# Expert job 0 in four quarter tiles with 32 slots, and its first three weight pieces in a buffer of their own

## The reference, cut to what matters

```python
def moe_swiglu(h, w_router, b_router, w_gate, w_up, w_down):
    logits = (h @ w_router).astype(jnp.float32) + b_router.astype(jnp.float32)
    top_vals, top_idx = lax.top_k(logits, TOP_K)
    top_w = jax.nn.softmax(top_vals, axis=-1)
    gates = jnp.sum(jax.nn.one_hot(top_idx, N_EXPERTS, dtype=jnp.float32)
                    * top_w[..., None], axis=-2).astype(h.dtype)
    out = jnp.zeros_like(h)
    for e in range(N_EXPERTS):
        out = out + gates[..., e:e + 1] * swiglu(h, w_gate[e], w_up[e], w_down[e])
    return out
```

## Time and profile before

| what | value |
|---|---|
| median of 3 runs | 1481.5 us (1481.41 to 1485.14) |
| profiled execution | 1486.44 us, span 1484.3 us |
| PE busy | 1399.5 us (94%) |
| DVE, ACT busy | 733.3 us (49%), 624.4 us (42%) |
| moved by DMA | 449.25 MB, mean 303 GB/s over the span |
| chain that ended last | PE 80%, DMA 8%, DVE 4%, ACT 3% |

### The profile page before, as it was taken

The page is one execution under the profiler, slowest core; times in us unless marked ns, Lnnn a source line. Parts: engine busy times, 40 slices in busy tenths (PEclk is TensorE's granted clock), DMA queues, the critical chain, the costliest instruction groups (busy, mean ns, idle before and its releaser), DMA issues.

```text
span 1484.3 us, 19444 instructions
## 1 busy us (share of the span) xinstructions
PE 1399.5 (94%) x7520; PEld 923.9 (62%) x7520; DVE 733.3 (49%) x923; ACT 624.4 (42%) x838; POOL 9.7 (1%) x24
## 2 busy tenths in 40 slices
PE   6988999999999988989999799999999999999987
PEld 5866788888789563347653276345876346876325
DVE  5665554444576355026620166206896108885005
ACT  5565544444473252026520155005775006774004
POOL 1000000000000000000000000000000000000000
PEclk9988999999999999999999999999999999999999
DMA  9922555555422385999879998999999999999992
GB/s 328 375 100 88 189 170 186 183 185 185 169 86 64 97 343 205 410 408 413 314 291 412 406 406 322 350 407 409 415 406 410 408 405 412 413 406 412 412 405 102
DMA packets 137356, 449.25 MB, mean 303 GB/s; under 512 B 8972, under 2 KB 13159, under 8 KB 124727
## 3 DMA queue, kind: packets, MB, share of 16 engines
q1 hardware_dynamic: 134736, 443.00, 77.9%
q0 software_dynamic: 1072, 3.84, 0.8%
q10 hardware_dynamic: 1462, 1.21, 0.3%
HBM read 441.27 MB, written 2.10 MB: 299 GB/s over the span
## 4 chain that ended last, share of the span: by engine, by line
PE 80%; DMA 8%; DVE 4%; ACT 3%; issue 2%; SPq 1%; ACTq 1%; DVEq 0%
PE psum L1006 18%; PE psum L587 18%; PE psum L589 17%; PE psum L588 17%; DMA weight_ring<-in_moe_w_gate 5%; DMA weight_ring<-in_ple_w_gate 2%; PE psum L1165 2%; DVE weight_lo L1810 1%; SPq L417 1%; PE psum L1180 1%; ACT weight_hi L1331 1%; ACTq L402 1%; DMA weight_ring<-in_attn_w_qkv 1%; PE psum L628 1%; PE psum L938 1%
## 5 line engine op out<-in xcount | busy, mean ns | idle before, releaser
L1331 ACT ACTIVATE weight_hi<-weight_ring 128x1024 fp32r<-128x1024 f32 x410 | 428.6, 1059 | 263.9 <-PE psum L589 242.2
L1810 DVE TENSOR_TENSOR weight_lo<-weight_ring,weight_hi 128x1024 fp32r<-128x1024 f32 x326 | 391.3, 1223 | 178.7 <-ACT weight_hi L1331 177.6
L1006 PE MATMUL psum<-weight_ring,silu_gate 128*64 128x512 f32 x960 | 216.7, 605 | 6.9 <-issue 6.3
L587 PE MATMUL psum<-weight_hi,act_hi 128*128 128x512 f32 x448 | 180.8, 403 | 11.2 <-issue 5.6
L588 PE MATMUL psum<-weight_lo,act_hi 128*128 128x512 f32 x448 | 178.3, 398 | 0.0
L589 PE MATMUL psum<-weight_hi,act_lo 128*128 128x512 f32 x448 | 178.1, 398 | 0.0
L2380 DVE TENSOR_TENSOR hidden<-silu_gate,psum 128x512 f32<-128x512 f32 (+1 forms) x20 | 12.4, 621 | 306.5 <-PE psum L1006 246.3
L1006 PEld LDWEIGHTS psum<-weight_ring,silu_gate 128*64 128x64 f32 x960 | 68.4, 139 | 139.4 <-issue 135.5
L587 PE MATMUL psum<-weight_hi,job_act_hi 128*128 128x512 f32 x336 | 137.9, 410 | 8.1 <-DVE weight_lo L1810 3.2
L589 PE MATMUL psum<-weight_hi,job_act_lo 128*128 128x512 f32 x336 | 134.3, 400 | 0.0
L588 PE MATMUL psum<-weight_lo,job_act_hi 128*128 128x512 f32 x336 | 134.1, 399 | 0.0
(11 more groups left out here) (353 smaller groups left out, 1397.8 us busy)
## 6 DMA issues: line engine op xcount, KB each, us to landing
weight_ring<-in_moe_w_gate SPq DMA_DIRECT2D x112, 1024.0 KB, 18.2
weight_ring<-in_moe_w_up SPq DMA_DIRECT2D x112, 1024.0 KB, 18.2
weight_ring<-in_moe_w_down SPq DMA_DIRECT2D x112, 1024.0 KB, 15.9
weight_ring<-in_ffn_w_gate SPq DMA_DIRECT2D x14, 1024.0 KB, 5.0
weight_ring<-in_ffn_w_up SPq DMA_DIRECT2D x14, 1024.0 KB, 5.0
weight_ring<-in_ffn_w_down SPq DMA_DIRECT2D x14, 1024.0 KB, 5.0
weight_ring<-in_attn_w_qkv SPq DMA_DIRECT2D x12, 1024.0 KB, 13.7
weight_ring<-in_conv_w_pw SPq DMA_DIRECT2D x12, 1024.0 KB, 5.1
```

The source lines that it names most:

```text
L587: pe.matmul(dst, ahi_, bhi_, start=first, stop=False, **kw)
L1006: ins = pe.matmul(ps[halves[half], bank, :], lhs, raw(u)[:, half * CW:(half + 1) * CW], start=first, stop=last)
L1331: act.activation(whi[:, u % SPLIT, :], raw(u), ACT.Copy).then_inc(hi_done, 1)
L1810: dve.tensor_tensor(wlo[:, u % SPLIT, :], raw(u), whi[:, u % SPLIT, :].bitcast(F32), ALU.subtract).then_inc(lo_done, 1)
```

## The change

Job 0 gets 32 slots (`EXTRA`) in place of 64. A unit is then four matmuls of 128x256 with 32 array columns each, in place of two of 128x512 with 64. The gather, the transposes, the activations and the job table follow the new width: what expert 0 has beyond 32 tokens becomes a job of its own, where it was what lies beyond 64. With 21 tokens for expert 0 the list of jobs stays as it was. `light_scatter(0, ...)` becomes `quarter_scatter`, with 16 matmuls of 32x256 in place of 8 of 64x512.

A second tile, `first_weights` (3 pieces), lies over the `weight_hi` and `weight_lo` buffers, which are idle between the last dense layer and the big job. Pieces 0 to 2 of job 0 go there instead of into the ring, and the ring starts with piece 3. So the ring's pieces 14 to 16 go to slots that were never filled, and wait for nothing of their own. SP issues the three `first_weights` DMAs behind ring piece 16 and ahead of piece 17.

```diff
-        emb1, = overlay(("embedding_1", [P, T, D], F32))
+        emb1, early = overlay(("embedding_1", [P, T, D], F32), ("first_weights", [P, EARLY, 2 * UNIT], F32))
...
             def load(piece, src, j, kt=4):
                 slot = piece % RING
-                if piece >= RING:
+                if j is None and U_MOE // 2 + RING <= piece < U_MOE // 2 + RING + EARLY:
+                    sp.sem_inc(piece_in[slot], 16)
+                elif piece >= RING:
                     sp.wait_ge(lo_done, after(2 * (piece - RING) + 2, JOB, j))
...
+            def first_weights(w):
+                sp.wait_ge(unit_used, U_PROJ1)
+                for i in range(EARLY):
+                    sp.dma_start(early[:, i, :].rearrange("p (t n) -> p t n", t=2),
+                                 w[i * 2 * P:(i + 1) * 2 * P, 0:GW].rearrange("(t p) n -> p t n", p=P)
+                                 ).then_inc(early_in[i], 16)
+
             def wide(at, w, s, j):
+                first = U_MOE // 2
                 for i in range(4):
-                    if j is None and at == U_MOE // 2 and i == X4_PIECE - U_MOE // 2:
+                    if j is None and at + i == first:
                         shifted_copies()
+                    if j is None and at + i < first + EARLY:
+                        continue
+                    if j is None and at + i == first + RING + EARLY:
+                        first_weights(w_first)
...
                 def wide_unit(u, lhs, bank, first, last):
                     wait_raw(u)
-                    for half in range(2):
-                        ins = pe.matmul(ps[halves[half], bank, :], lhs, raw(u)[:, half * CW:(half + 1) * CW],
+                    for g, rows in enumerate(tiles):
+                        ins = pe.matmul(ps[rows, bank, 0:width], lhs, weights(u)[:, g * width:(g + 1) * width],
                                         start=first, stop=last)
                     ins.then_inc(lo_done, 1)
...
+            def quarter_scatter(done, banks):
+                pe.wait_ge(ylo_done, 2 * done + 2)
+                for odd in range(2):
+                    if odd:
+                        pe.wait_ge(sc_first, 1)
+                    for t in range(T):
+                        for q in (odd, odd + 2):
...
-            light_job(0, embedding=True)
+            light_job(0, embedding=True, slots=EXTRA)
```

More of the change, by code:

```diff
@@ L209, in program @@
         piece_in = [sem(f"piece_in{i}") for i in range(RING)]
+        early_in = [sem(f"first_weights_in{i}") for i in range(EARLY)]
         hi_done = sem("hi_done")
@@ L940, in gather_rows @@
                     last.then_inc(rows_ready, 2)
+                elif slots == EXTRA:
+                    for t in range(T):
+                        for q in range(NQ):
+                            last = pe.matmul(ps[q * EXTRA:(q + 1) * EXTRA, bank, 0:HW], sel[:, t, 0:EXTRA],
+                                             hrow[:, t, q * HW:(q + 1) * HW], start=t == 0, stop=t == T - 1)
+                    last.then_inc(rows_ready, 2)
                 else:
@@ L959, in _ @@
             pe.wait_ge(sel_done, 1)
-            gather_rows(LIGHT, 2)
-            gather_transpose(LIGHT, 2, 0, None)
+            gather_rows(EXTRA, 2)
+            pe.wait_ge(rows_done, 2)
+            for k in range(2):
+                last = pe.transpose(ps[:, 2, k * P:(k + 1) * P], rows_x[:, k * P:(k + 1) * P], ident[:, :])
+            last.then_inc(xe_ready, 2)
             pe.sem_inc(ghT_ready, GROUPS)
@@ L1012, in narrow_unit @@
                     for k in range(2):
-                        for half in range(2):
-                            at = k * CW + half * HW
-                            ins = pe.matmul(ps[halves[half], bank, 0:HW], xe[:, 2 * i + k, :], raw(u)[:, at:at + HW],
+                        for g, rows in enumerate(tiles):
+                            n = CW // parts
+                            at = k * CW + g * n
+                            ins = pe.matmul(ps[rows, bank, 0:n], acts[:, 2 * i + k, :], weights(u)[:, at:at + n],
                                             start=i + k == 0, stop=i == 3 and k == 1)
@@ L1021, in light_linear @@
                         if s < 3:
-                            wide_unit(first + unit + i, xe[:, i, :], bank, i == 0, i == KT - 1)
+                            wide_unit(first + unit + i, acts[:, i, :], bank, i == 0, i == KT - 1)
                         else:
@@ L1077, in light_job @@
                         t, half = n % 2, n // 2
-                        pe.matmul(ps[:, n, :], selT[halves[half], t * P:(t + 1) * P],
-                                  ysb[halves[half], 0:CW], start=True, stop=True).then_inc(sc_ready, 1)
+                        pe.matmul(ps[:, n, :], selT[tiles[half], t * P:(t + 1) * P],
+                                  ysb[tiles[half], 0:CW], start=True, stop=True).then_inc(sc_ready, 1)
             def small_job(j):
@@ L1640, in _, with light_job @@
             act.sem_inc(ghThi_done, GROUPS)
-            def light_job(j, last_job=False, between=False, embedding=False):
+            def light_job(j, last_job=False, between=False, embedding=False, slots=LIGHT):
                 first = U_MOE + (HALF if between else 0)
```

75 lines of the change are left out of this document (52 added, 23 removed).

## The result

The change makes the kernel slower. The first timing has a median of 1501.2 us in four executions (1494.3, 1500.1, 1502.3, and a disturbed one of 1768 that the ratio leaves out) against 1481.9 us: 1.0095, 95% interval [1.0066, 1.0124]. The ratios come from all undisturbed executions and are not the quotients of the medians. Three later timings of the same two kernels give 1493.6 against 1485.5 (1.0058 [1.0043, 1.0074]), 1495.0 against 1484.5 (1.0075 [1.006, 1.009]) and 1494.3 against 1484.3 (1.0058 [1.0038, 1.0078]). The forecast was 1488.1, +0.45%, with a range that ended at 1492.0. Direction and mechanism were right, the size too small, and all four medians are above the range.

A forecast was written before the change was run, and what follows sets the result against it. The prediction took the DMA stream, not PE, to set the end of job 0. It added 6.4 us for the later stream and 0.2 for the scatter, +6.6 on the median, giving 1488.1 us (+0.45%), range 1483.0 to 1492.0.

The forecast's parts named there:

- What bounds job 0: Job 0: the DMA stream sets its end, at 2.60 us a piece, not PE, which takes 1.76 us a piece.
- Seven pieces behind the wait: Start of job 0: SP issues seven pieces at 566.7, first_weights last, landing 581.6 to 590.9; piece 17 issued at 594.8.
- From piece 17 to the big job: Rest of job 0: the same 25 pieces at 2.60 us; piece 42 lands at 664.5, big job starts at 667.1.
- What the quarter tiles save counts as zero: Job 0: 38 us of PE time saved lies beside a stream that PE waits for, so it gains nothing.
- Scatter: Job 0's scatter, where PE is the bound: one added PE wait between two halves, +0.2 us (0.1 to 1.2).
- The shift is passed on whole: Behind job 0: all waits are relative, so the later start reaches the kernel's end unchanged, nothing added.
- The base: Whole kernel: the sum was put on the median of the runs, 4.9 us below the profiled execution of 1486.4.
- the term for the stream: Start of job 0: piece 17 lands at 599.6 instead of 593.2, +6.4 us.
- Rival 1: Start of job 0: same step but smaller, clock high or store out of the way sooner; +2 to +4.4 us, 1485; chance 0.18.
- Rival 2: Job 0: PE bounds it after all, so 38 us are saved less 8.8 of later start; 1452; chance 0.02.
- Rival 3: Start of job 0: the early fetch works, landing ahead of 572.8; piece 17 lands 4.5 us sooner, 1477; chance 0.06.
- Rival 4: Job 0: clock stays low throughout, PE falls behind the landings; +11.6 us, 1493.1; chance 0.10.

The follow-up runs named there:

- the quarter tiles alone: The changed kernel with pieces 0 to 2 left in the ring (no early fetch): 1484.1 against 1485.5 us for the kernel before, 0.9998.
- the fillers: Changed kernel plus an unused 128x256 matmul behind each wide unit from job 0's second up stage: 1494.2 us, 1.0069; in two tile-used-twice variants 1482.8 and 1477.6.
- half tiles with early fetch: The kernel before, job 0 still with 64 slots, its first three pieces in first_weights issued behind ring piece 16: 1491.1 against 1485.5 us, 1.0044.

## Why the prediction was right or wrong

**What bounds job 0: right.** The stream sets its end. With quarter tiles the third window above has DMA share 1.03 beside a PE that is busy two thirds of the time.

**Seven pieces behind the wait: right, nearly to the tenth.** T is 0.9 us later than before in this profile. Counted from T of each profile, E0 was forecast at +15.5 and landed at +16.4 (10.9 us behind piece 13 for four pieces, 2.7 each and not 2.56), E2 at +24.8 and +25.0, piece 17's issue at +28.7 in both. The store took 6.1 - 2.5 = 3.6 us of E2's time, inside its bounds; this offset most of what E0 lost. The clock read 0.50 over all four units after E2, as I took it.

**From piece 17 to the big job: right, 0.8 us short.** Piece 17 took 5.1 us to land and not 4.8, and the 25 pieces behind it 65.5 and not 64.9. In the profile on which the sum was made this gives +7.2, over six profiles 7.3 to 7.9, mean 7.5, for a forecast of **6.4: this term was 1.1 too small.** The big job starts 2.6 us behind piece 42, as today.

**What the quarter tiles save counts as zero: right** for the changed kernel; alone they bring piece 42 3.3 us sooner. PE waits for DMAs in every piece, as forecast.

**Scatter: 0.2 forecast, 0.3 measured.** The changed kernel's PE timeline from its first matmul to the next group (670.64 to 671.79, 1.15 us, in the earlier trace rows):

```profile
678.51 0.39 PE L1029 MATMUL psum<-expert_out_hi,one_hot_T_r 32*128 32x256 f32 x2
...
679.32 0.39 PE L1029 MATMUL psum<-expert_out_hi,one_hot_T_r 32*128 32x256 f32 x2
...
679.99 0.41 PE L1225 MATMUL psum<-weight_ring,extra_act 128*32 128x256 f32 x2
```

1.48 us, in two halves of 0.81 and 0.67 us, the wait for the drain in the first.

**"The shift is passed on whole": a step that failed.** Big job to end is 823.2 on the mean of three profiles before and 824.8 on that of six of the changed kernel, +1.6, of which the scatter is 0.3; T itself is 565.7 on the mean of both. Of the rest, 1.0 is the slip of 3 us in two of six profiles; some tenths have no name. With 7.5 that makes 9.1, against 8.1, 10.6 and 10.0 us in the three later timings.

**The base.** The sum on the profiled execution was 1493.0, and the changed kernel's profiled execution took 1494.3. It was set down by 4.9 us to the median of three runs, and later medians of the kernel before lie 3 to 4 us above that. Of the 5.5 to 6.9 us by which the later timings miss 1488.1, this is about half.

**The steps that failed, together.** The base was 2.8 to 4.0 us too low, the term for the stream 1.1 too small (7.5 for 6.4), and "passed on whole" left out 1.4 behind job 0 (1.6 for the scatter's 0.2): 5.3 to 6.5 us, where the later timings miss the forecast by 5.5 to 6.9. The first timing misses it by 13 us. The two terms explain 2.5 of these and the base at most 4; the rest stays open.

**The rivals.** Rival 1 (+2 to +4.4) falls by the profile: the clock was not high when E2 landed. Rival 2 falls by the quarter tiles alone. The Trainium skill, "TensorEngine Tiling (Array Packing)", Theoretical Speedup, gives twice the speedup for 32 that it gives for 64, and the trace agrees on the price of the work (ten units in 4.52 us at full clock, 0.45 each for 0.88), but the kernel got no shorter by it. Rival 3 names what the change could do, and did when its three DMAs were put ahead of piece 13: T + 85.3, 6.6 sooner than before, where it had 4.5; 3.3 of these are the quarter tiles', and 3.4 us showed in the time. Rival 4 falls by the profile (PE waits for DMAs up to its last units) and by the fillers, though the clock went low again and again, as it supposed. The Trainium skill, "TensorE: Matmul & The Clock Gate", HAM oscillation, tells of a kernel whose waits for DMAs send the clock low again and again; the forecast found no such pattern in the trace, and the changed kernel has one, with waits of 0.5 to 1.7 us. Windows of it:

```profile
616.50:623.00 6.50, 4.54 (x40) 1.67 (x44) 0.00 (x0) 0.38 (x1) 0.00 (x0) 0.50 1.01 420
623.50:630.00 6.50, 2.48 (x40) 0.83 (x32) 0.00 (x0) 0.00 (x0) 0.00 (x0) 1.00 1.01 407
630.20:636.80 6.60, 5.36 (x48) 1.67 (x48) 0.00 (x0) 0.00 (x0) 0.00 (x0) 0.50 1.03 405
```

It costs next to nothing (0.4 us at piece 42, by the fillers): even at 0.50 two units take 1.93 us, and a piece takes 2.56.

**Still open.** What the first timing's executions of 1500.1 and 1502.3 did: no profile is of one like them. The mean clock of the second (0.957) is lower than that of any later execution (0.963 and up). Whether the slip at the first small job comes from the change. And what the early fetch, put ahead of piece 13, gives in half tiles: every kernel with the better order had quarter tiles, so their share in it (3.3 us at piece 42) is known from the run of quarter tiles alone.

## What to carry to other kernels

A buffer that is free early gives an early load only if nothing that waits stands ahead of it in the list of the engine that issues it; here, in quarter tiles, the same three DMAs cost 10.8 us behind a waiting one (99.4 for 88.6 to piece 42) and gave 3.3 ahead of it (85.3). Where loads set the end of a stage, count pieces and landings first, and ask of the arithmetic only when it frees a buffer: 38 us of matmul time saved there brought the last landing 3.3 us forward and gave no time that could be measured. And put a sum on the time of the execution it was read from, unless there are more than three runs to tell where the median lies.

## What the runs showed of the hardware

The clock of TensorE read 0.50 for 12.25 us of work in bursts (7.6 us busy) after a wait of 14 us; it read 0.97 on the mean of the next 5 us, while PE worked through the ring's resident pieces. In half tiles with early fetch, after a wait of 12.7 us, PE was busy for 6.5 of the next 7.5 us, and the clock read 1.00 from there on. An engine kept at work to the end of job 0 found the clock at 1.00 at the big job's first matmul in five profiles (half tiles with early fetch, and fillers), and one that had waited for each of its last pieces found 0.50 there in all others. The kernel before, too, had 0.50 there, after a wait of 3.0 us, though PE was busy for 63.5 of 64.8 us ahead of it; the half tiles with early fetch waited 1.4 us.

A store of 1 MB from SBUF in the middle of a saturated stream of loads delayed the next landing by 3.0 to 3.8 us in the six profiles of the changed kernel, by 4.1 to 4.5 in the three of the kernel before, and by 2.5 and 2.6 in the two of half tiles with early fetch; a load of the same size takes 2.56.
